# Head of a two-layer hybrid trunk: the first modulation computed in two halves by channels

## The chip, the cores and the metric

One core of a Trainium2 chip runs the whole program. The metric is the device time of one execution in microseconds (us). The kernel before took 1956.28 us, the median of 3 runs (1955.67 to 1959.99).

## The reference

Two groups of tokens (128 context tokens, 512 latent tokens, 1024 channels each) go through two layers with the same weights. Every layer first normalizes and modulates its input; the modulation comes from a small matrix product with a vector per group. Cut to what the change touches:

```python
for i in range(DEPTH):
    m = jax.nn.silu(cvec) @ P['ada_w'][i] + P['ada_b'][i]          # 1024 -> 6 * 1024
    sh1, sc1, g1, sh2, sc2, g2 = jnp.split(m[:, None, :], N_MOD, axis=-1)
    h = rmsnorm(x, P['norm_mix_g'][i]) * (1 + sc1) + sh1
    if i % 2 == 0:                                                 # layer 0: SSD || short convolution
        y, st = mixer_ssd_conv(h, P, e, h0)                        # u = h @ ssd_w_in, dt among its columns
    else:                                                          # layer 1: neighbourhood attention
        ...
    x = x + g1 * y
    h = rmsnorm(x, P['norm_ffn_g'][i]) * (1 + sc2) + sh2
    x = x + g2 * conv_ffn(h, P, i)
```

Nothing of layer 0's mixer can start before `sh1` and `sc1` of layer 0 are there: the first two sections of `ada_w[0]`, 1024 rows by 2048 columns of 4 bytes, 8.4 MB.

## The kernel before, in words

The activations lie in SBUF by channels: `C` = 8 chunks of 128 channels (the partitions) by `T` = 644 columns (128 context tokens, 4 columns of padding, 512 latent tokens). Every product with a large weight is done in three matmuls on a high and a low part: ScalarE copies a weight slot `raw` (128 x 1024) into `w_hi` (`split`, line 1087), GpSimd subtracts to get `w_lo` (`low`, line 550), and TensorE runs, for each chunk k and each half of the 644 columns, `w_hi*act_hi`, `w_hi*act_lo` and `w_lo*act_hi` (`half_slot`, lines 607, 608, 611). `raw` has two buffers, `w_hi` and `w_lo` four slots. The order of the work of each engine is written out by hand, with semaphores between the engines.

The head of the program runs so. SyncE's queue loads twelve small parameter arrays, then the eight row blocks of the first two sections of `ada_w`, 128 rows x 2048 columns each, into the tiles `first` (line 383), seven of them at once, since there are seven tiles. The eighth waits until TensorE is through with the first. Behind it the queue has the first two slots of `ssd_w_in` (`raw`, line 360), the table `na_rpb`, and the spill of `x`. ScalarE's queue loads the tokens `tok`, the dt weights `wdt`, and three small vectors `dtb`, `dld`.

TensorE transposes the tokens into PSUM in eight steps (lines 701, 702); VectorE copies each step to `x` (lines 1499, 1500). ScalarE has squared the tokens meanwhile and takes the roots; VectorE inverts them. `norm_spread(0)` (lines 657, 660) spreads the inverses over the partitions, and ScalarE copies them to `rinv` (line 1113). TensorE then sums the modulation over the eight blocks, four groups of 32 array columns at a time (line 707, bank 7). ScalarE copies the sums to `arow` (line 1166), TensorE turns them into columns (line 714), and VectorE adds the bias, `mod`, and forms `scale_a` (lines 1548, 1551).

VectorE had normalized all eight chunks before (`xn`, line 1511), added `dskip` (line 1515) and made the `masks` for the attention of layer 1 (lines 1519 to 1531). Then the eight chunks are modulated: for each, ScalarE writes `act_hi` (line 1169, two pieces, one for each group of tokens), and the unrounded value goes to `nt`, by VectorE for the even chunks (line 1561) and by ScalarE for the odd ones (line 1169); VectorE subtracts to get `act_lo` (line 1567). TensorE follows chunk by chunk: six matmuls for dt (lines 724 to 726) and six for the first tile of `ssd_w_in` (slot 0). ScalarE splits slots 0 and 1 between the chunks and slots 2 and 3 behind them.

Behind the chunks TensorE does tiles 1, 2 and 3 (slots 1 to 3). A tile goes into one of two pairs of PSUM banks, so tile 3 needs the banks of tile 1, which ScalarE frees (`tile_free1`) with the second of its two copies of tile 1 in `conv_in` (lines 1194, 1195). ScalarE takes these after tile 0's convolution: `zs` (line 1197) waits for VectorE's convolution of tile 0 (lines 1684, 1685), and VectorE comes to it only after it has built the table `tab` (15 copies, line 1654) and computed dt by a series (lines 1661 to 1677).

The names that matter below: `first_summed` (sums of the blocks done), `first_copied`, `first_turned`, `mod_ready`, `scale_ready`; `x_scaled` (a chunk of `xn` is there); `act_high`, `nt_ready`, `act_ready` (a chunk is ready for TensorE); `low_split` (a slot's `w_lo` is there).

## Time and profile before

| | us |
|---|---|
| median of 3 runs (lowest, highest) | 1956.28 (1955.67, 1959.99) |
| the profiled execution, own time | 1957.59 |
| its span in the profile | 1955.8 |
| TensorE busy in it | 1895.7 (97%) |
| VectorE, ScalarE, GpSimd busy | 1031.5, 672.0, 634.9 |
| mean granted TensorE clock | 0.985 of full |

All times of a row are counted from the start of the profiled span. In a row of a timeline the first number is the start, the second the time from the start of the first instruction to the end of the last of the row, and in square brackets stands how long the engine was idle before it and what ended that. Matmuls are pipelined, so a row's time is longer than the distance to the next row's start. The granted clock is 1.00 at 2.4 GHz and 0.50 at 1.2 GHz. The span is divided by the page into 40 slices of 49 us; everything that the change touches lies in the first two.

### The profile page before, as it was taken

The numbers are of one execution on the slowest core, as the hardware profiler recorded it, in microseconds if no ns is written. First come the engines' busy times: TensorE is split into PE (matmuls) and PEld (weight loads), VectorE is DVE, ScalarE is ACT, GpSimd is POOL, SyncE is SP. The second block draws the span as 40 slices with busy tenths as digits, with TensorE's granted clock in tenths as the row PEclk, the third lists the DMA queues.
The fourth block names the chain that finished last, engine by engine and source line by source line (L and its number), as shares of the span: only waits on it lengthen the run. The fifth ranks groups of instructions, "written<-read, shape, count | busy, mean of one in ns | idle before, by whom it ended". The sixth has DMA issues, their size and how long they took to land.

```text
span 1955.8 us, 35222 instructions
## 1 busy us (share of the span) xinstructions
PE 1895.7 (97%) x13425; PEld 1813.6 (93%) x13425; DVE 1031.5 (53%) x1987; ACT 672.0 (34%) x1021; POOL 634.9 (32%) x309
## 2 busy tenths in 40 slices
...
DMA packets 272884, 192.48 MB, mean 98 GB/s; under 512 B 25370, under 2 KB 259222, under 8 KB 271270
## 3 DMA queue, kind: packets, MB, share of 16 engines
...
## 4 chain that ended last, share of the span: by engine, by line
PE 86%; issue 5%; ACT 2%; DVE 2%; POOL 2%; DMA 2%; SPq 0%; POOLq 0%; ACTq 0%; DVEq 0%
PE ps L607 25%; PE ps L611 25%; PE ps L608 25%; PE ps L679 2%; POOL w_lo L550 2%; PE ps L1034 1%; PE ps L1014 1%; PE ps L856 1%; PE ps L999 1%; DVE act_lo L1595 1%; ACT sp L1386 1%; PE ps L686 0%; DMA x<-x_spill 0%; PE ps L1053 0%; PE ps L841 0%
## 5 line engine op out<-in xcount | busy, mean ns | idle before, releaser
L550 POOL TENSOR_TENSOR w_lo<-raw,w_hi 128x1024 fp32r<-128x1024 f32 x244 | 598.6, 2456 | 1229.6 <-ACT w_hi L1087 1229.6
L607 PE MATMUL ps<-act_hi,w_hi 128*128 128x322 f32 x2752 | 847.3, 315 | 6.6 <-DVE act_lo L1595 2.6
L608 PE MATMUL ps<-act_lo,w_hi 128*128 128x322 f32 x2624 | 802.4, 312 | 0.0
L611 PE MATMUL ps<-act_hi,w_lo 128*128 128x322 f32 x2752 | 635.6, 312 | 0.0
L607 PEld LDWEIGHTS ps<-act_hi,w_hi 128*128 128x128 f32 x2752 | 524.9, 191 | 20.4 <-issue 14.6
L608 PEld LDWEIGHTS ps<-act_lo,w_hi 128*128 128x128 f32 x2624 | 498.2, 190 | 0.0
L611 PEld LDWEIGHTS ps<-act_hi,w_lo 128*128 128x128 f32 x2752 | 465.8, 189 | 0.0
L1087 ACT ACTIVATE w_hi<-raw 128x1024 fp32r<-128x1024 f32 x244 | 256.1, 1051 | 370.2 <-PE ps L611 327.2
L607 PE MATMUL ps<-f_hi,w_hi 128*128 128x322 f32 x704 | 214.2, 311 | 0.0
L608 PE MATMUL ps<-f_lo,w_hi 128*128 128x322 f32 x704 | 213.7, 310 | 0.0
L1886 DVE SCALAR_TENSOR_TENSOR x<-ps,mod,x 128x128 f32 (+1 forms) x144 | 54.4, 433 | 265.8 <-PE ps L611 265.2
L611 PE MATMUL ps<-f_hi,w_lo 128*128 128x322 f32 x704 | 161.9, 311 | 0.0
L607 PEld LDWEIGHTS ps<-f_hi,w_hi 128*128 128x128 f32 x704 | 133.5, 190 | 0.0
L608 PEld LDWEIGHTS ps<-f_lo,w_hi 128*128 128x128 f32 x704 | 132.8, 189 | 0.0
L1685 DVE SCALAR_TENSOR_TENSOR ft<-fg,par,ft 128x644 f32<-128x644 f32 x44 | 123.6, 2810 | 7.8 <-DVE ft L1684 7.5
L611 PEld LDWEIGHTS ps<-f_hi,w_lo 128*128 128x128 f32 x704 | 118.0, 188 | 0.0
L1923 DVE TENSOR_TENSOR fg<-ps,spread 128x644 f32<-128x644 f32 x44 | 36.5, 830 | 132.2 <-PE ps L611 121.8
L1346 ACT ACTIVATE fe<-ft,gb 128x130 f32<-128x130 f32 x88 | 44.9, 557 | 127.4 <-DVE ft L1685 127.4
L1342 ACT ACTIVATE ft<-fg,par 128x644 f32<-128x644 f32 x44 | 36.7, 834 | 127.4 <-DVE fg L1923 127.3
L1495 DVE TENSOR_TENSOR acc<-acc,sq 128x644 f32<-128x644 f32 x40 | 58.2, 1455 | 19.9 <-ACT sq L1098 19.9
L1684 DVE SCALAR_TENSOR_TENSOR ft<-fg,par,ft 128x644 f32<-128x644 f32 x44 | 43.3, 984 | 44.3 <-ACT ft L1342 43.8
L1350 ACT ACTIVATE f_hi<-fa 128x644 f32 x44 | 32.7, 743 | 95.1 <-DVE fa L1935 95.1
...
## 6 DMA issues: line engine op xcount, KB each, us to landing
...
raw<-in_ssd_w_in SPq DMA_DIRECT2D x44, 512.0 KB, 3.8
raw<-in_ffn_w_gate SPq DMA_DIRECT2D x44, 512.0 KB, 3.7
raw<-in_ffn_w_up SPq DMA_DIRECT2D x44, 512.0 KB, 3.7
...
raw<-in_na_w_qkv SPq DMA_DIRECT2D x24, 512.0 KB, 3.7
...
first<-in_ada_w SPq DMA_DIRECT2D x8, 1024.0 KB, 13.0
```

The lines of the kernel that those rows point to most:

```text
L550: g.tensor_tensor(w_lo[:, s], raw[:, s % RAW], w_hi[:, s], ALU.subtract).then_inc(S["low_split"], 1)
L607: t.matmul(out, hi, chunk_of(src_hi, k0 + k, cols), start=start, stop=False)
L608: t.matmul(out, hi, chunk_of(src_lo, k0 + k, cols), start=False, stop=False)
L611: mm = t.matmul(ps[:, 2 * tset + h, 0:HALF], lo, chunk_of(src_hi, k0 + k, cols), start=False, stop=stop)
L679: mm = t.matmul(ps[g:g + ADA_COLS, bank, :], csil_w[:, 2 * q + k, :], ada[:, k, b * ADA_N:b * ADA_N + ADA_N], start=(q == 0), stop=(q == A ...
L1087: a(w_hi[:, s], raw[:, s % RAW], ACT.Copy).then_inc(S["high_split"], 1)
L1342: a(ft[k][:], fg[k][:, 1:T + 1], ACT.Copy, scale=w1).then_inc(S["ffn_mid"], 1)
L1346: ins = a(fe[k][:, lo:hi], ft[k][:, lo:hi], ACT.Gelu_apprx_tanh, bias=gb[:, k, stream:stream + 1])
L1495: tt(acc[:], acc[:], sq[:], ALU.add).then_inc(S["squares_used"], 1)
L1684: st.then_wait(stt(dst[:], buf[:, 0:T], w[:, bass.ds(w0, 1)], dst[:], ALU.mult, ALU.add))
L1685: return stt(dst[:], buf[:, 2:T + 2], w[:, bass.ds(w2, 1)], dst[:], ALU.mult, ALU.add)
L1886: ins = stt(dst, ps[:, 2 * k + bank, lo:hi], gate, dst, ALU.mult, ALU.add)
```

## The change

The two sections are taken in two halves by channels: columns 0 to 511 of both sections first, then columns 512 to 1023. Each of the seven tiles `first` would hold two half blocks (`quarters`); one tile is dropped, so there are twelve places. SyncE's queue loads eight half blocks of half 0 (128 partitions x 2 runs of 512 elements), then slot 0 of `ssd_w_in`, then eight half blocks of half 1 (the last four wait for the first sums), then slot 1.

On TensorE, `first_sum(0, s)` stands behind each of the eight steps of transposition, `norm_spread(0)` and `first_turn(0)` behind them. The loop over the chunks begins once half 0 of the modulation is there; the sums of half 1 stand behind chunks 0, 1 and 2 (three, three, two), and `first_turn(1)` behind chunk 3. Chunk 4 waits for `mod_ready`.

On ScalarE the copy of half 0's sums comes before `inverse(0)`, then the split of slot 0, then chunks 0 to 3; at chunk 4 the copy of half 1's sums, the split of slot 1, and chunks 4 to 7. The exponential of `dtb`, with the load of its table, moves from ahead of the chunks to behind them, before the splits of slots 2 and 3.

On VectorE `half_modulation` does `mod` and `scale_a` of four chunks at a time, into bank 4's columns; `xn` is no longer made for all chunks ahead but one chunk ahead of its use, inside the loop. `dskip` moves behind the chunks (before `tab`), the masks behind the first four convolutions.

```diff
-        first += [nc.alloc_sbuf_tensor_at(f"first{5 + n}", [P, 4, ADA_N], F32, offset=first_lo_at + n * 2 * C * P * 4) for n in range(2)]
+        first += [nc.alloc_sbuf_tensor_at("first5", [P, 4, ADA_N], F32, offset=first_lo_at + 2 * C * P * 4)]
+        quarters = [f[:, 2 * q:2 * q + 2, :] for f in first for q in range(2)]
...
-            for n in range(C):
-                if n >= len(first):
-                    sp.wait_ge(S["first_summed"], n - len(first) + 1)
-                sp.dma_start(first[n % len(first)][:], ada_w[0, n * P:n * P + P, 0:4 * ADA_N].rearrange("p (b n) -> p b n", b=4)
-                             ).then_inc(S[f"first_loaded{n}"], 16)
-            for s in range(RAW):
+            for n in range(2 * C):
+                if n == C:
+                    weights(SLOT_IN, 0, 0, rows(w_in, 0, C, U_BC))
+                if n >= len(quarters):
+                    sp.wait_ge(S["first_summed"], n - len(quarters) + 1)
+                src = bass.AP(tensor=ada_w.tensor, offset=(n % C) * P * MODS * D + (n // C) * ADA_N, ap=[[MODS * D, P], [D, 2], [1, ADA_N]])
+                sp.dma_start(quarters[n % len(quarters)], src).then_inc(S[f"first_loaded{n}"], 16)
+            for s in range(1, RAW):
...
+            def first_sum(half, k):
+
+                n = half * C + k
+                pe.wait_ge(S[f"first_loaded{n}"], 16)
+                for b in range(4):
+                    cols = slice(b % 2 * 2 * P, b % 2 * 2 * P + 2 * P)
+                    mm = t.matmul(ps[ADA_COLS * b:ADA_COLS * b + ADA_COLS, 3 if half else 7, 0:2 * P], csil_w[:, k, :],
+                                  quarters[n % len(quarters)][:, b // 2, cols], start=(k == 0), stop=(k == C - 1))
+                mm.then_inc(S["first_summed"], 1)
+
+            def first_turn(half):
+
+                pe.wait_ge(S["first_copied"], half + 1)
+                picks = ident[:].rearrange("p (b q) -> p b q", b=4)[:, :, 0:2]
+                for n in range(2):
+                    mm = t.matmul(ps[:, 4, 16 * half + 8 * n:16 * half + 8 * n + 8], arow[:, (2 * half + n) * P:(2 * half + n) * P + P], picks,
+                                  start=True, stop=True)
+                mm.then_inc(S["first_turned"], 1)
+
             for s in range(C):
                 if s >= 2:
                     pe.wait_ge(S["x_copied"], s - 1)
                 for n in range(LC):
                     t.transpose(ps[:, 5 + s % 2, n * P:n * P + P], tok[:, n, s * P:s * P + P], ident[:])
                 t.transpose(ps[:, s % 2, 0:P], tok[:, LC, s * P:s * P + P], ident[:]).then_inc(S["x_transposed"], 1)
+                first_sum(0, s)
             norm_spread(0)
-            for n in range(C):
-                pe.wait_ge(S[f"first_loaded{n}"], 16)
-                for b in range(4):
-                    mm = t.matmul(ps[ADA_COLS * b:ADA_COLS * b + ADA_COLS, 7, :], csil_w[:, n, :], first[n % len(first)][:, b, :],
-                                  start=(n == 0), stop=(n == C - 1))
-                mm.then_inc(S["first_summed"], 1)
-            pe.wait_ge(S["first_copied"], 1)
+            first_turn(0)
             pe.wait_ge(S["x_copied"], C)
-            picks = ident[:].rearrange("p (b q) -> p b q", b=4)[:, :, 0:2]
-            for n in range(4):
-                mm = t.matmul(ps[:, 5, 8 * n:8 * n + 8], arow[:, n * P:n * P + P], picks, start=True, stop=True)
-            mm.then_inc(S["first_turned"], 1)
-
-
             pe.wait_ge(S["wdt_ready"], 1)
-            pe.wait_ge(S["mod_ready"], 1)
             for k in range(C):
+                if k == 1:
+                    pe.wait_ge(S["rinv_ready"], 1)
                 pe.wait_ge(S["act_ready"], k + 1)
+                if k == C // 2:
+                    pe.wait_ge(S["mod_ready"], 1)
                 for h in range(2):
                     out, cols = ps[0:2 * HEADS, 5 + h, 0:HALF], slice(h * HALF, h * HALF + HALF)
                     t.matmul(out, wdt_hi[:, k, :], chunk_of(act_hi, k, cols), start=(k == 0), stop=False)
@@ -729,6 +744,10 @@
                 if k == 0:
                     slot_ready(SLOT_IN, 0, 0)
                 mm = half_slot(0, 0, [k], act_hi, act_lo, k == 0, k == C - 1)
+                for n in ((0, 1, 2), (3, 4, 5), (6, 7), ())[k] if k < 4 else ():
+                    first_sum(1, n)
+                if k == C // 2 - 1:
+                    first_turn(1)
...
+            act.wait_ge(S["first_summed"], C)
+            a(arow[:, 0:2 * P], ps[:, 7, 0:2 * P], ACT.Copy).then_inc(S["first_copied"], 1)
             inverse(0)
-            act.wait_ge(S["dskip_loaded"], 48)
-            a(dtb[:, 1, :], dtb[:, 1, :], ACT.Exp).then_inc(S["a_exp"], 1)
-            act.wait_ge(S["first_summed"], C)
-            a(arow[:], ps[:, 7, :], ACT.Copy).then_inc(S["first_copied"], 1)
+            split(SLOT_IN, 0, 0)
 
             def first_piece(dst, c, lo, hi, stream):
                 return a(dst, xn[:, c * T + lo:c * T + hi], ACT.Identity, scale=scale_a[:, c, stream:stream + 1],
                          bias=mod[:, 0, c, stream:stream + 1])
 
             for c in range(C):
-                if c == 0:
-                    act.wait_ge(S["scale_ready"], 1)
-                    act.wait_ge(S["x_scaled"], C)
+                if c == C // 2:
+                    act.wait_ge(S["first_summed"], 2 * C)
+                    a(arow[:, 2 * P:4 * P], ps[:, 3, 0:2 * P], ACT.Copy).then_inc(S["first_copied"], 1)
+                    for s in range(1, RAW):
+                        split(SLOT_IN, 0, s)
+                if c % (C // 2) == 0:
+                    act.wait_ge(S["half_ready"], c // (C // 2) + 1)
+                act.wait_ge(S["x_scaled"], c + 1)
                 for lo, hi, stream in STREAMS:
                     ins = first_piece(act_hi[:, c * T + lo:c * T + hi], c, lo, hi, stream)
                 ins.then_inc(S["act_high"], 1)
                 if c % 2 == 0:
                     if c > 0:
                         act.wait_ge(S["act_ready"], c)
+                    act.wait_ge(S["x_scaled"], c + 2)
                     for lo, hi, stream in STREAMS:
                         ins = first_piece(nt[:, 1, lo:hi], c + 1, lo, hi, stream)
                     ins.then_inc(S["nt_ready"], 1)
-                if c < RAW:
-                    split(SLOT_IN, 0, c)
+            act.wait_ge(S["dskip_loaded"], 48)
+            a(dtb[:, 1, :], dtb[:, 1, :], ACT.Exp).then_inc(S["a_exp"], 1)
...
-            for c0 in range(C):
-                tt(xn[:, c0 * T:c0 * T + T], x[:, c0 * T:c0 * T + T], rinv[:], ALU.mult).then_inc(S["x_scaled"], 1)
-            dve.wait_ge(S["dskip_loaded"], 48)
-            for h in range(2):
-                hp = slice(64 * h, 64 * h + 64)
-                ins = tt(dskip[hp, :], dld[hp, 0, h::2], dld[hp, 1, h::2], ALU.add)
-            st.did(ins)
-
...
-            st.wait()
-            dve.wait_ge(S["first_turned"], 1)
-            turned = ps[:, 5, 0:32].rearrange("p (n m h s) -> p m h n s", n=4, m=2, h=2)
-            for m in (1, 0):
-                adab = par[:, R_ADAB + m * C:R_ADAB + m * C + C].rearrange("p (h n) -> p h n", h=2).unsqueeze(3).broadcast_to([P, 2, 4, 2])
-                ins = tt(mod[:, m].rearrange("p (h n) s -> p h n s", h=2), turned[:, m], adab, ALU.add)
-                if m == 1:
-                    st.then_wait(ins)
-                    st.did(stt(scale_a[:], mod[:, 1], 1.0, bcast(par[:, R_NMIX:R_NMIX + C], 2, [P, C, 2]), ALU.add, ALU.mult))
-            ins.then_inc(S["mod_ready"], 1)
-            dve.wait_ge(S["mod_ready"], 1)
-            st.wait()
-            dve.sem_inc(S["scale_ready"], 1)
+            def half_modulation(half):
+
+                dve.wait_ge(S["first_turned"], half + 1)
+                turned = ps[:, 4, 16 * half:16 * half + 16].rearrange("p (n m h s) -> p m h n s", n=2, m=2, h=2)
+                at_ = slice(C // 2 * half, C // 2 * half + C // 2)
+                for m in (1, 0):
+                    adab = par[:, R_ADAB + m * C:R_ADAB + m * C + C][:, at_].rearrange("p (h n) -> p h n", h=2).unsqueeze(3).broadcast_to([P, 2, 2, 2])
+                    ins = tt(mod[:, m, at_].rearrange("p (h n) s -> p h n s", h=2), turned[:, m], adab, ALU.add)
+                    if m == 1:
+                        st.then_wait(ins)
+                        st.did(stt(scale_a[:, at_], mod[:, 1, at_], 1.0, bcast(par[:, R_NMIX:R_NMIX + C][:, at_], 2, [P, C // 2, 2]), ALU.add, ALU.mult))
+                if half == 1:
+                    dve.sem_inc(S["scale_ready"], 1)
+                    ins.then_inc(S["mod_ready"], 1)
+                    dve.wait_ge(S["mod_ready"], 1)
+                else:
+                    st.did(ins)
+                st.wait()
+                dve.sem_inc(S["half_ready"], 1)
+
+            def scaled_x(c):
+
+                tt(xn[:, c * T:c * T + T], x[:, c * T:c * T + T], rinv[:], ALU.mult).then_inc(S["x_scaled"], 1)
+
+            scaled_x(0)
             for c in range(C):
+                if c % (C // 2) == 0:
+                    half_modulation(c // (C // 2))
                 if c % 2 == 0:
                     if c > 0:
                         dve.wait_ge(S["act_ready"], c - 1)
+                    dve.wait_ge(S["x_scaled"], c + 1)
                     for lo, hi, stream in STREAMS:
                         st.did(ts(nt[:, 0, lo:hi], xn[:, c * T + lo:c * T + hi], scale_a[:, c, stream:stream + 1],
                                   mod[:, 0, c, stream:stream + 1], ALU.mult, ALU.add))
+                    scaled_x(c + 1)
                     st.wait()
                 else:
+                    if c < C - 1:
+                        scaled_x(c + 1)
                     dve.wait_ge(S["nt_ready"], c // 2 + 1)
...
             new_sum()
 
+            dve.wait_ge(S["dskip_loaded"], 48)
+            for h in range(2):
+                hp = slice(64 * h, 64 * h + 64)
+                ins = tt(dskip[hp, :], dld[hp, 0, h::2], dld[hp, 1, h::2], ALU.add)
+            st.did(ins)
+
             st.then_wait(v.memset(tab[:], 0.0))
...
             dve.wait_ge(S["sums_exp"], 1)
             st.did(tt(sc[:, :, K_END, :], sc[:, :, K_END, :], sc[:, :, K_DT, :], ALU.mult))
+            dve.wait_ge(S["consts_ready"], 2)
+            st.then_wait(v.tensor_single_scalar(qi[:, 0:1], qi[:, 0:1], QW - 1, ALU.bitwise_and))
...
+                st.then_wait(stt(masks[:, n, :], dist, float(QW - 1), ok, ALU.is_le, ALU.mult))
+                ins = ts(masks[:, n, :], masks[:, n, :], 1.0, BIG, ALU.subtract, ALU.mult)
+                st.did(ins)
+            st.wait()
```

## Rows read from the trace of the kernel before

**Rows 1.** The page: the chain that ended last, shares of the span by engine.

```profile
PE 86%; issue 5%; ACT 2%; DVE 2%; POOL 2%; DMA 2%; SPq 0%; POOLq 0%; ACTq 0%; DVEq 0%
```

**Rows 2.** Tile `first`: its DMA issues (duration ns, first and last start) and landings.

```profile
L383 SPq DMA_DIRECT2D first<-in_ada_w x8: 328/451/506, 6.1 to 25.2; - x8
...
DMA to landing us min/median/max: 7.6/13.0/20.3
```

**Rows 3.** DMA issues of 0 to 45 us: count, KB each, median us to landing.

```profile
raw<-in_ssd_w_in SPq DMA_DIRECT2D x3, 512.0 KB, 9.9
...
wdt<-in_ssd_w_in ACTq DMA_DIRECT2D x1, 128.0 KB, 22.9
```

**Rows 4.** Timeline of TensorE, 14 to 41 us.

```profile
22.25 0.66 PE L701 MATMUL ps<-ident,tok 128*128 128x128 f32 x4 [0.92 <-DVE x L1500]
...
23.07 1.06 PE L660 MATMUL ps<-ident,roots 128*128 128x128 f32 x8
24.06 6.35 PE L707 MATMUL ps<-first,csil_w 128*32 128x512 f32 x56
33.91 1.93 PE L707 MATMUL ps<-first,csil_w 128*32 128x512 f32 x8 [3.50 <-DMA first<-in_ada_w]
36.55 1.88 PE L714 MATMUL ps<-ident,arow 128*128 128x8 f32 x8 [0.72 <-ACT arow L1166]
```

**Rows 5.** Timeline of TensorE's weight loads, 24 to 38 us.

```profile
24.05 0.16 PEld L707 LDWEIGHTS ps<-first,csil_w 128*32 128x32 f32 x8
```

**Rows 6.** Windows: length, busy us (count) of PE, PEld, DVE, ACT, POOL; granted clock, DMA share, GB/s.

```profile
33.90:38.00 4.10, 3.38 (x15) 1.65 (x15) 2.32 (x13) 0.60 (x1) 0.00 (x0) 0.50 1.12 427
49.00:50.00 1.00, 1.00 (x6) 0.92 (x6) 1.00 (x3) 0.08 (x1) 0.00 (x0) 0.66 0.94 244
```

**Rows 7.** Timeline of VectorE, 24 to 130 us.

```profile
25.88 6.01 DVE L1511 TENSOR_TENSOR xn<-x,rinv 128x644 f32<-128x644 f32 x8 [0.23 <-ACT rinv L1113]
32.28 0.34 DVE L1515 TENSOR_TENSOR dskip<-dld 64x8 f32<-64x8 f32 x2 [0.39 <-DMA dld<-in_ssd_d]
...
38.55 0.17 DVE L1548 TENSOR_TENSOR mod<-ps,par 128x16 f32<-128x16 f32 x1 [1.97 <-PE ps L714]
...
39.20 0.80 DVE L1561 TENSOR_SCALAR nt<-xn,scale_a,mod 128x128 f32<-128x128 f32 x2 [0.18 <-DVE mod L1548]
...
43.57 1.93 DVE L1567 TENSOR_TENSOR act_lo<-nt,act_hi 128x644 fp32r<-128x644 f32 x1 [2.30 <-ACT act_hi L1169]
...
55.59 0.83 DVE L1567 TENSOR_TENSOR act_lo<-nt,act_hi 128x644 fp32r<-128x644 f32 x1 [0.86 <-ACT act_hi L1169]
...
58.25 4.08 DVE L1654 COPY tab<-tabr 16x31 f32<-16x31 f32 x15
...
99.99 0.89 DVE L1684 SCALAR_TENSOR_TENSOR cgs<-gpad,halfw,cgs 128x644 f32<-128x644 f32 x1 [6.35 <-ACT gpad L1195]
```

**Rows 8.** Timeline of GpSimd, 24 to 130 us.

```profile
42.46 5.27 POOL L550 TENSOR_TENSOR w_lo<-raw,w_hi 128x1024 fp32r<-128x1024 f32 x2 [38.80 <-ACT w_hi L1087]
```

**Rows 9.** Timeline of ScalarE, 24 to 130 us.

```profile
25.26 0.59 ACT L1113 ACTIVATE rinv<-ps 128x512 f32<-128x512 f32 x1
25.86 1.28 ACT L1164 ACT_TABLE_LOAD   x1
...
39.14 1.20 ACT L1169 ACTIVATE act_hi<-xn,mod,scale_a 128x128 fp32r<-128x128 f32 x2 [2.64 <-DVEq L1555]
...
41.33 1.04 ACT L1087 ACTIVATE w_hi<-raw 128x1024 fp32r<-128x1024 f32 x1
...
74.37 0.70 ACT L1195 ACTIVATE gpad<-ps 128x644 f32<-128x644 f32 x1
```

**Rows 10.** Timeline of TensorE, 40 to 130 us.

```profile
44.87 0.63 PE L607 MATMUL ps<-act_hi,w_hi 128*128 128x322 f32 x1 [1.66 <-POOL w_lo L550]
...
60.98 0.41 PE L607 MATMUL ps<-act_hi,w_hi 128*128 128x322 f32 x1
...
75.32 0.31 PE L607 MATMUL ps<-act_hi,w_hi 128*128 128x322 f32 x1
```

28 lines of the change are left out of this document (12 added, 16 removed).

## Prediction

> **What bounds the kernel now.** I read the page's chain first: 86% of it is TensorE [rows 1], so a head that ends earlier is worth something only if TensorE's unbroken run of tiles starts earlier. Next the loads. Seven row blocks of 1 MB are queued from 6.1 us, one every 0.45 us; the first lands 7.6 us after its issue (13.7), the seventh 20.3 after (29.1) [rows 2], so one MB takes 2.6 us, and the eighth ends TensorE's wait at 33.9 [rows 4]. Then the engines of the head: the sums take 1.93 us, the turn 1.88 [rows 4], VectorE's first modulation comes at 38.55 [rows 7], chunk 0's `act_hi` at 39.14 [rows 9], TensorE's first tile at 44.87 [rows 10]. The reader is to see that the eighth block sets all this.
>
> Then I ask what the run behind hangs on. The last chunk's `act_lo` ends at 55.59 + 0.83 = 56.42 [rows 7], tile 1 starts at 60.98 and tile 3 at 75.32 [rows 10], 7.17 us a tile, 0.149 us a matmul. Tile 3 needs tile 1's banks, which ScalarE's copy frees at 74.37 + 0.70 = 75.07 [rows 9]: only 0.25 us before TensorE wants them. That copy stands behind VectorE's chain: last `act_lo`, the table's copies (to 58.25 + 4.08 = 62.33 [rows 7], 5.91 us behind that `act_lo`), dt, the convolution of tile 0. So two paths arrive together at 75.1 to 75.3, and the one over VectorE has nearly no slack. The change pays only where it brings the last `act_lo` forward.
>
> **Loads and sums of half 0.** Half blocks are 0.5 MB, 1.3 us each; eight land by 13.7 - 1.3 + 7 x 1.3 = 21.5. I take 22.5 for the eighth, since runs of 2 KB have no row here; bounds 21.5 and 25. Slot 0 follows with 0.5 MB: 24 to 25.
>
> The sums of half 0 move between the transpositions. Seven blocks took 6.35 us [rows 4], 0.9 each with the drain and a short wait counted in; I take 0.86 at full clock and twice that at half (the eighth: 1.93 with its drain). Its eight weight loads issue in 0.16 us [rows 5], so loads do not set its pace, columns do, and a half block costs 0.43 or 0.86; bounds 0.2 and 0.9. Eight add 4.3 to the transpositions, partly in waits that were there (0.92 before the last step [rows 4]). I take +1.3 (bounds 0 and 4.5): the last sum ends at 24.15 instead of the transpositions at 22.85. `norm_spread` takes 1.3, to 25.3, and `first_turn(0)`, four records of the eight in 1.88, 0.5 at full clock: 25.8. `rinv` is there 0.65 us behind the spread [rows 9], 25.95.
>
> wdt lands 22.9 us after its issue, at 24.8, though it is 128 KB [rows 3]: it shares the DMA engines with row blocks whose runs are 8 KB. ScalarE copies it ahead of half 0's sums. With it landing at 24.8 again, the turn ends 0.3 later, and that is the bound I keep. The Trainium skill (DMA: Bandwidth & Descriptors, Queues, rings and completion order) has each engine go round its queues a packet at a time. By that wdt would land earlier beside runs of 2 KB, and those 0.3 us go.
>
> **Chunks 0 to 3.** VectorE: `xn` of chunk 0 takes 0.75 (6.01 for eight [rows 7]), 26.0 to 26.75; half 0's modulation to 27.3. ScalarE splits slot 0 from 26.0 to 27.0 (1.04 [rows 9]), and GpSimd subtracts for about 2.4 us, to 29.45. While GpSimd did that before (42.46 to 47.73 [rows 8]) VectorE's `act_lo` took 1.93 instead of 0.83 [rows 7]: the one waits for the other. So `nt` of chunk 0 starts at 29.45: 0.80 + 0.75 (`xn` of chunk 1) + 0.8 = 31.8, and TensorE starts at 31.9 with slot 0 there, 9.5 us before dt's first matmul and 13 before tile 0's.
>
> But it starts at the low clock. A pause of 3.5 us before 33.91 left the granted clock at 0.50 [rows 4, 6]; here it is 25.8 to 31.9. Before, from the start at 44.87 the clock came back within 49 to 50, whose mean is 0.66 [rows 6]: at 49.7, 4.8 us. I take 4.8 again. In them go chunk 0's twelve matmuls (12 x 0.27 = 3.2) and 1.9 half blocks of sums; at full clock remain 36 x 0.149 = 5.4 and 6.1 x 0.43 = 2.6. End of chunk 3: 31.9 + 4.8 + 8.0 = 44.7, the last sum 1.8 before, 42.9. Half 1 has landed by about 34, so it does not bind; VectorE's chunks 1 to 3 (2.3 us each with `xn` among them) are ready by 39, and don't either.
>
> **The second modulation** is the new wait. `first_turn(1)` 0.5, to 45.2; the first add 0.17 [rows 7]. Meanwhile ScalarE: copy of the sums 0.35, split of slot 1 1.04, to 44.3, and GpSimd holds 44.4 to 46.8. `scale_a` reads two operands from SBUF and falls in there. I let it wait: half 1 ready at T = 47.1. No row shows so small an instruction in this place; bounds T = 46.0 (not held) and 47.1. The Trainium skill (SBUF — State Buffer, SBUF: two separate sides) says that a VectorE instruction with both inputs in SBUF fully blocks while a GpSimd one that reads SBUF runs, and that one reading PSUM is not held; by it the add passes and `scale_a` waits, T = 47.1, and a VectorE free of it would give 46.0, 1.1 us less on the whole. The 1.93 us row agrees for the long ones.
>
> **Chunks 4 to 7.** Per pair VectorE has `nt` 0.80 and `xn` 0.75; then ScalarE, which waits for that `xn`, does `nt` and `act_hi` of the odd chunk, 1.1 each (two pieces in 1.20 with the drain [rows 9]), and `act_lo` 0.85: 4.65. Two pairs: the last `act_lo` ends at T + 9.3 = 56.4, against 56.42. TensorE, idle from 45.2 to T + 2.4 = 49.5, is at the low clock once more and ends tile 0 near 59; ScalarE has exponential, table load 1.28 [rows 9] and splits 2 and 3 to 59.1, then dt's copy, so tile 1 starts near 60.4, 0.6 earlier than now.
>
> **Moved pieces.** The masks leave VectorE's stretch between 32.62 and 36.58 (3.96 us, the idle 1.97 before 38.55 counted off [rows 7]), where they lay under the loads: gain 0. They go into 6.35 us of idle before the convolution at 99.99 [rows 7]: 0, and 2.4 to spare; if that cover shrank below 3.96 the difference would hit the convolutions. `dskip` goes onto VectorE's chain: +0.34 [rows 7]. The table load leaves a stretch in the loads' shadow and delays splits 2 and 3 by 1.5; slot 2 is wanted at 67: 0. SP's queue: slot 0 passes eight half blocks (it lands at 25 instead of 35), slot 1 none; the spill of `x` behind them waits for nobody.
>
> **Sum.** VectorE's path: 0.0 + 0.34; the banks of tile 1 come at 75.4. TensorE's path wants them at 74.7, and waits. Tile 3 at 75.4 instead of 75.32: +0.1. Made against the profiled execution, 1957.59 becomes 1957.7; against the median 1956.28, 1.3 below that execution, it is 1956.4. The lead of 9 to 13 us at chunk 0 is spent on sums among the chunks, `xn` inside the loop (a pair 4.65 instead of 3.3 of ScalarE alone), and a second stop of about 4 us for the second modulation.
>
> **Rivals.** (a) *Second modulation early*: `scale_a` isn't held, TensorE's clock is up by 35. T = 44.9 to 45.5, change 0.34 - 1.9 - 0.25: -1.8, 1954.5. For it: pauses so far differ. Against: the low clock behind 3.5 us of pause. (b) *The lead is handed on*: slot 0's subtraction and the clock both cost nothing, chunk 3 ends at 31 + 10.5 = 41.5, T = 42: last `act_lo` 51.3, -4.8, 1951.5. Against: rows 7 and 8. (c) *Slower, by the clock*: with the matmuls of chunks 0 to 3 all at half pace, 12.9 + 6.9 = 19.8 us, chunk 3 ends at 51.7, T = 52.2 to 54.2 and the gate moves +5.5 to +7: 1962.5. It decides against me once the clock stays down past about 41, nine us after the start. Against: 4.8 us before. (d) *Slot 0 is late*: before, the slots landed 9.9 us (median) after issue [rows 3]. ScalarE's split stands ahead of chunk 0, so if slot 0 lands at 31 or later instead of 25, all of it moves by 5: +5, 1961.4; then the change doesn't do what it says.
>
> **Chances.** Forecast 0.65 (own range 1955 to 1959.5: bounds of the sums, half blocks and T), a 0.14, b 0.07, c 0.08, d 0.06. The range for 8 in 10 is 1953.6 to 1960.2. About 0.2%, 3.9 us, is what a measurement of this kernel tells from no change, so faster means under 1952.4 and slower over 1960.2: faster is b and a little of a, 0.09; slower c and most of d, 0.13; same 0.78.
>
> **What would show it.** Right: half 0's last sum near 24; dt's first matmul at 31 to 33; granted clock 0.50 there and full by 38; TensorE idle about 4 us behind chunk 3; `scale_a` of half 1 as GpSimd's subtraction ends; last `act_lo` at 56 to 57; TensorE idle a moment before tile 3, released by ScalarE's copy. Wrong: a last `act_lo` before 53 or past 60, tile 3 away from 75.4 by over 3 us, or a convolution behind tile 4 that waits for masks.

## The result, and the profile after

The changed kernel is slower: 1965.68 us (median of 7 runs, 1960.6 to 1967.22) against 1957.78 (median of 7, 1955.67 to 1959.99) for the kernel before in the same session, ratio 1.0037 with a 95% interval of 1.0027 to 1.0048. The forecast was 1956.4, the range 1953.6 to 1960.2, so the time lies outside it, on the side that had a chance of 0.13. The profiled execution took 1965.73 us, its span is 1963.9, and TensorE was busy for 1897.0 us of it, 1.3 more than before: the other 6.8 of the 8.1 us are idle time of TensorE. The chain of the page is again TensorE's.

The landing of the first small loads, which TensorE's first matmul waits for, moves from run to run (11.58 to 12.39 us into the span over 19 profiles; 11.67 in the profile before, 12.39 in this one). So where two kernels are compared I count from that first matmul ("behind the first matmul").

The page's chain of the kernel after, the issues of DMAs of 0 to 45 us (count, KB each, median us to landing) and the landings of tile `first` [rows 1, 3, 2]:

```profile
PE 87%; issue 5%; DVE 2%; POOL 2%; ACT 2%; DMA 1%; SPq 0%; POOLq 0%; ACTq 0%; DVEq 0%
```

```profile
raw<-in_ssd_w_in SPq DMA_DIRECT2D x3, 512.0 KB, 12.4
...
wdt<-in_ssd_w_in ACTq DMA_DIRECT2D x1, 128.0 KB, 14.8
```

```profile
DMA to landing us min/median/max: 7.5/10.9/13.7
```

The loads bound nothing, as forecast: wdt came 14.8 us behind its issue instead of 22.9, and nothing in this head waited for it or for a half block. That queues are served in turn is what the Trainium skill (DMA: Bandwidth & Descriptors, Queues, rings and completion order) says; by that rule wdt had to come earlier beside shorter runs, and the trace agrees. The losses start on TensorE. Its timeline after [rows 4, 10]:

```profile
24.97 0.64 PE L707 MATMUL ps<-first,csil_w 128*32 128x256 f32 x8
...
26.23 0.64 PE L707 MATMUL ps<-first,csil_w 128*32 128x256 f32 x8
...
28.02 0.51 PE L716 MATMUL ps<-ident,arow 128*128 128x8 f32 x4
...
34.35 0.45 PE L739 MATMUL ps<-act_hi,wdt_hi 128*32 128x322 f32 x1 [5.82 <-DVE act_lo L1585]
...
37.67 2.42 PE L707 MATMUL ps<-first,csil_w 128*32 128x256 f32 x24
...
45.23 1.07 PE L707 MATMUL ps<-first,csil_w 128*32 128x256 f32 x16
...
48.03 0.51 PE L716 MATMUL ps<-ident,arow 128*128 128x8 f32 x4
52.80 0.33 PE L739 MATMUL ps<-act_hi,wdt_hi 128*32 128x322 f32 x1 [4.26 <-DVE act_lo L1585]
...
63.24 0.49 PE L756 MATMUL ps<-ident,dtrow 32*128 32x32 f32 x5 [1.13 <-ACT dtrow L1226]
...
80.41 0.49 PE L611 MATMUL ps<-act_hi,w_hi 128*128 128x322 f32 x1 [2.21 <-ACT gpad L1219]
```

A step of five transpositions and four sums repeats every 1.265 us (23.70, 24.97, 26.23) with no idle between. Then come the two stops, 5.82 and 4.26 us, both released by VectorE's `act_lo`, and a third of 2.21 us ahead of tile 3, released by ScalarE's copy, where the kernel before had none [rows 10]. VectorE, GpSimd and ScalarE after [rows 7 to 9]:

```profile
30.18 2.54 DVE L1576 TENSOR_SCALAR nt<-xn,scale_a,mod 128x128 f32<-128x128 f32 x2 [0.15 <-DVE mod L1550]
...
48.58 0.17 DVE L1550 TENSOR_TENSOR mod<-ps,par 128x8 f32<-128x8 f32 x1 [7.08 <-PE ps L716]
48.78 1.36 DVE L1553 SCALAR_TENSOR_TENSOR scale_a<-mod,par 128x8 f32<-128x8 f32 x1
...
59.27 0.83 DVE L1585 TENSOR_TENSOR act_lo<-nt,act_hi 128x644 fp32r<-128x644 f32 x1 [1.75 <-ACT act_hi L1187]
...
60.81 0.34 DVE L1672 TENSOR_TENSOR dskip<-dld 64x8 f32<-64x8 f32 x2
61.40 0.86 DVE L1675 MEMSET tab<- 16x960 f32 x1 [0.25 <-issue]
62.29 5.23 DVE L1678 COPY tab<-tabr 16x31 f32<-16x31 f32 x15
...
106.77 0.89 DVE L1708 SCALAR_TENSOR_TENSOR cgs<-gpad,halfw,cgs 128x644 f32<-128x644 f32 x1 [4.13 <-ACT gpad L1219]
```

```profile
29.84 2.34 POOL L554 TENSOR_TENSOR w_lo<-raw,w_hi 128x1024 fp32r<-128x1024 f32 x1 [26.17 <-ACT w_hi L1106]
47.77 2.35 POOL L554 TENSOR_TENSOR w_lo<-raw,w_hi 128x1024 fp32r<-128x1024 f32 x1 [15.59 <-ACT w_hi L1106]
61.74 4.74 POOL L554 TENSOR_TENSOR w_lo<-raw,w_hi 128x1024 fp32r<-128x1024 f32 x2 [11.62 <-ACT w_hi L1106]
```

```profile
59.18 1.28 ACT L1210 ACT_TABLE_LOAD   x1
...
60.61 1.99 ACT L1106 ACTIVATE w_hi<-raw 128x1024 fp32r<-128x1024 f32 x2
62.51 0.68 ACT L1226 ACTIVATE dtrow<-ps 32x644 f32<-32x644 f32 x1
...
79.57 0.70 ACT L1219 ACTIVATE gpad<-ps 128x644 f32<-128x644 f32 x1
```

The reader is to lay the three over one another. GpSimd runs from 29.84, 47.77 and 61.74; in each of these stretches VectorE has an instruction that is far too long: `nt` 2.54 instead of 0.80, `scale_a` 1.36 instead of 0.17, and the 15 copies of the table 5.23. That the add of `mod` at 48.58 took 0.17 beside GpSimd while `scale_a` behind it was held agrees with the Trainium skill (SBUF — State Buffer, SBUF: two separate sides) on one and two operands from SBUF. The number of operands does not tell it all: `nt` and the table's copies read one tile each in SBUF and were held too, 2.54 us instead of 0.80 and 5.23 instead of the 1.35 that they take with GpSimd idle (below). For comparison, GpSimd's pair of subtractions behind the last chunk in the kernel before, where the last `act_lo` ends at 56.42 [rows 7]:

```profile
56.52 4.76 POOL L550 TENSOR_TENSOR w_lo<-raw,w_hi 128x1024 fp32r<-128x1024 f32 x2 [8.78 <-ACT w_hi L1087]
```

It starts 0.10 us behind that `act_lo`; in the changed kernel the pair starts at 61.74, 1.64 behind an `act_lo` that ends at 60.10.

The granted clock (columns as in rows 6):

```profile
80.41:84.41 4.00, 4.00 (x17) 4.00 (x18) 3.16 (x3) 1.51 (x2) 0.85 (x1) 0.57 0.45 122
...
34.30:39.00 4.70, 4.65 (x28) 3.19 (x32) 3.74 (x7) 3.30 (x7) 0.00 (x0) 0.50 1.13 396
39.00:44.00 5.00, 5.00 (x57) 3.05 (x50) 1.49 (x2) 1.57 (x3) 0.00 (x0) 0.94 0.98 393
52.80:57.00 4.20, 4.20 (x18) 3.40 (x19) 3.19 (x6) 2.81 (x6) 0.00 (x0) 0.59 0.12 35
```

It is low behind both long stops, as forecast, and low once more, 0.57 over four us, behind the third; four us behind the start of tile 3 have 1.00 in the kernel before.

### The profile page after: what moved, and what is told of

The parts are those of the page before. It is cut to its first block, busy times and chain, and to the rows that moved or that the text cites. A ratio compares the mean times of both kernels' runs of the same rounds, so it can differ in the third digit from the quotient of the medians.

```text
span 1963.9 us, 35373 instructions
## 1 busy us (share of the span) xinstructions
PE 1897.0 (97%) x13489; PEld 1813.8 (92%) x13489; DVE 1033.1 (53%) x1990; ACT 672.5 (34%) x1022; POOL 634.9 (32%) x309
## 4 chain that ended last, share of the span: by engine, by line
PE 87%; issue 5%; DVE 2%; POOL 2%; ACT 2%; DMA 1%; SPq 0%; POOLq 0%; ACTq 0%; DVEq 0%
PE ps L611 25%; PE ps L615 25%; PE ps L612 25%; PE ps L683 2%; POOL w_lo L554 2%; PE ps L1053 1%; PE ps L1033 1%; PE ps L875 1%; PE ps L1018 1%; DVE act_lo L1613 1%; ACT sp L1410 1%; PE ps L707 1%; DMA x<-x_spill 1%; PE ps L690 0%; PE ps L795 0%
```

## The experiments

Two points hold for all. "The gate" is ScalarE's copy of tile 1's banks, which frees them for tile 3. Positions in the table are us behind the first matmul of each profile; each kernel was timed against the kernel before in turns, in 5 rounds, or 3 for the first four; `before_p1`, `before_p2`, `after_p1` and `after_p2` are single profiles. The first four columns come from one profile each, the ratio from all executions, and an execution that was profiled can stand at either end of its kernel's times: that of `warm` took 1961.9 (median 1958.78), that of `sums_early` 1958.25 (median 1961.67).

| kernel | last `act_lo` ends | table's copies take | tile 3 starts | idle ahead of it | ratio, 95% interval |
|---|---|---|---|---|---|
| before; before_p1; before_p2 | 44.75; 43.58; 42.83 | 4.08; 4.14; 4.09 | 63.65; 62.43; 62.22 | 0; 0.19; 0 | 1 |
| after | 47.71 | 5.23 | 68.02 | 2.21 | 1.0037 (1.0027, 1.0048) |
| after_again | 47.37 | 5.24 | 67.69 | 2.25 | 1.0045 (1.0031, 1.0059) |
| after_p1; after_p2 | 47.16; 47.67 | 5.21; 5.23 | 67.47; 67.99 | 2.20; 2.22 | |
| before_late | 43.47 | 1.35 | 63.99 | 1.86 | 1.0017 (1.0007, 1.0027) |
| tab_idle | 47.03 | 1.35 | 65.62 | 0.49 | 1.0029 (1.0018, 1.0040) |
| warm | 46.04 | 5.22 | 66.34 | 2.19 | 1.0014 (1.0003, 1.0025) |
| sums_early | 45.29 | 5.23 | 65.61 | 2.25 | 1.0026 (1.0016, 1.0035) |
| second_fast | 42.87 | 5.23 | 63.19 | 2.21 | 1.0008 (0.9999, 1.0017) |
| no_table | 41.68 | 1.35 | 59.87 | 1.04 | 0.9996 (0.9987, 1.0005) |
| no_table_warm | 41.67 | 1.35 | 59.86 | 1.04 | 0.9993 (0.9983, 1.0002) |
| before_tab_moved | 44.71 | 1.35 | 63.63 | 0 | 0.9999 (0.9990, 1.0008) |
| after_tab_moved | 47.71 | 1.35 | 66.31 | 0.49 | 1.0023 (1.0012, 1.0033) |
| sums_behind | 47.11 | 5.24 | 67.43 | 2.22 | 1.0036 (1.0024, 1.0049) |
| exp_idle | 48.27 | 1.36 | 68.52 | 2.36 | 1.0035 (1.0021, 1.0049) |
| exp_dskip_idle | 48.28 | 4.09 | 67.09 | 1.94 | 1.0038 (1.0026, 1.0050) |

**Is it the gate?** The first two runs load and unload VectorE's chain and leave the rest alone. `before_late` repeats the clear of the table four times; `tab_idle` does the table ahead of the second modulation, where VectorE waits 7.08 us.

```diff
-            st.then_wait(v.memset(tab[:], 0.0))
+            for _ in range(5):
+                st.then_wait(v.memset(tab[:], 0.0))
```

> The kernel before, with four more clears of `tab` (0.86 us each, 3.5 us in all) on VectorE ahead of the table's copies; nothing else. Theory G: the gate has 0.25 us of slack there, so tile 3 starts 3.2 us later (78.5 instead of 75.3 us), TensorE idles just before it, released by ScalarE's copy to `gpad`, and perhaps runs on at the low clock for some us (up to 1.6 more): 1961.0 to 1962.6 against 1957.8. Rival W: VectorE has room there, the time stays at 1957.8.

```diff
+                if c == C // 2:
+                    st.then_wait(v.memset(tab[:], 0.0))
+                    dve.wait_ge(S["table_loaded"], 16)
+                    for r in range(DR):
+                        st.did(v.tensor_copy(tab[:, DR - 1 - r, QW:QW + DC], tabr[:, r, DC - 1::-1]))
                 if c % (C // 2) == 0:
                     half_modulation(c // (C // 2))
...
-            st.then_wait(v.memset(tab[:], 0.0))
-            for r in range(DR):
-                st.did(v.tensor_copy(tab[:, DR - 1 - r, QW:QW + DC], tabr[:, r, DC - 1::-1]))
```

> The changed kernel, with the table for the attention (the clear of `tab` and its 15 copies) built in VectorE's idle stretch ahead of the second half's modulation (41.5 to 48.5 us in the changed kernel) instead of behind the last chunk. Theory G (the gate): tile 3 of the input product starts when ScalarE has freed tile 1's banks, and that stands behind VectorE's last `act_lo`, the table and dt. Without the table's 6.3 us on that path tile 3 should start when TensorE itself comes to it, at 78.1 instead of 80.4 us, without the 2.2 us of idle and without the low clock behind it (1.6 us): 3.9 us less than the changed kernel, 1961.8. Rival W (work): TensorE's own longer head sets the end, and VectorE's order is cover; then tile 1 and tile 3 start where they do now and the time stays at 1965.7.

VectorE, GpSimd and TensorE of `before_late`:

```profile
61.93 1.35 DVE L1655 COPY tab<-tabr 16x31 f32<-16x31 f32 x15
```

```profile
55.75 4.74 POOL L550 TENSOR_TENSOR w_lo<-raw,w_hi 128x1024 fp32r<-128x1024 f32 x2 [8.78 <-ACT w_hi L1087]
```

```profile
76.17 0.39 PE L607 MATMUL ps<-act_hi,w_hi 128*128 128x322 f32 x1 [1.86 <-ACT gpad L1195]
```

4.45 us of clears gave 1.86 us of idle and a ratio of 1.0017: slower, but less than expected (1959.93 us against 1961.0 to 1962.6). The reason is in the rows: the copies began behind GpSimd's end (55.75 + 4.74 = 60.49) and took 1.35 instead of 4.08, so the chain grew by 4.45 - 2.73 = 1.7. This is the first sight of what the copies cost: alone 1.35. In `tab_idle` they took 1.35 too, tile 3 came 1.9 to 2.4 us earlier than in the profiles of the changed kernel, and of the idle 0.49 was left; its median, 1961.57, is the 1961.8 that was expected. Both agree with the gate, and with a time that follows it.

**Where does the chain lose?** `warm` puts transpositions of the identity (46 behind `first_turn(0)`, 34 behind `first_turn(1)`), whose results nobody reads, into the two stops, so that the clock stays up. `sums_early` takes half 1's sums four and four behind chunks 0 and 1, and its turn behind chunk 2.

```diff
             first_turn(0)
+            filler(46)
...
                     first_turn(1)
+                    filler(34)
```

> The changed kernel, with transpositions of the identity into an unused part of bank 7 as filler in TensorE's two pauses (46 behind the first turn, 34 behind the second), to keep its clock up. Theory G with the low clock as one of its parts: chunk 0 to 3 run at the full clock from the start, 2.3 us shorter, the second half's modulation, the last `act_lo` and the gate come 2.3 us earlier (tile 3 at 78.1), and the time is 1963.4. Rival D (VectorE and ScalarE pace chunks 0 to 3, the clock is only a symptom): chunk 3 ends less than 1 us earlier and the time stays above 1965. A second pause before tile 3 stays in either case.

```diff
-                for n in ((0, 1, 2), (3, 4, 5), (6, 7), ())[k] if k < 4 else ():
+                for n in ((0, 1, 2, 3), (4, 5, 6, 7), (), ())[k] if k < 4 else ():
...
-                if k == C // 2 - 1:
+                if k == C // 2 - 2:
```

> The changed kernel, with the eight sums of half 1 behind chunks 0 and 1 (four each) instead of 0, 1 and 2, and the second turn behind chunk 2 instead of chunk 3, so that chunk 3's matmuls lie beside the second modulation. Half 1's last block lands at about 37 us and is needed at 43. Theory G: the half's modulation, the last `act_lo` and tile 3 come 1.7 us earlier, the idle before chunk 4 shrinks from 4.3 to about 2.5 us, and the time is 1964.0 or, where the shorter pause also keeps the clock up, 1963. Rival W: TensorE does the same work in another order, tile 1 starts when it does now, 1965.7.

`warm` brought the last `act_lo` 1.1 to 1.7 us forward, and its time came down by more than that (1958.78, against 1963.4 expected); where the rest of it comes from is not shown. `sums_early` brought it 1.9 to 2.4 forward (1961.67, against 1963 to 1964). In both the idle ahead of tile 3 stayed at 2.2: the gate keeps its distance to the last `act_lo`. ScalarE's copy ends 20.2 us behind it, and tile 3 starts 20.3 behind it, in each of the profiles of the changed kernel and of these two; in the three of the kernel before the copy ends 18.7 behind it, and tile 3 starts 0.1 to 0.7 after the copy. `after_again` is the changed kernel once more.

> The changed kernel, unaltered, for its time beside the same runs of the kernel before as the three that follow, and for a second profile. Both theories: 1.0037 times the kernel before; tile 3 starts 68 us after TensorE's first matmul, with about 2 us of idle ended by ScalarE's copy to `gpad`. A profile whose head differs by over 1 us in that distance would say that single profiles don't carry differences of that size.

It gave 1.0045, tile 3 at 67.69. `second_fast` adds to `sums_early` the split of slot 1 ahead of the wait for half 1's sums, so that GpSimd does not hold `scale_a`, and `xn` of chunks 5 to 7 in VectorE's idle.

```diff
+                    for s in range(1, RAW):
+                        split(SLOT_IN, 0, s)
                     act.wait_ge(S["first_summed"], 2 * C)
                     a(arow[:, 2 * P:4 * P], ps[:, 3, 0:2 * P], ACT.Copy).then_inc(S["first_copied"], 1)
-                    for s in range(1, RAW):
-                        split(SLOT_IN, 0, s)
...
+                if c == C // 2:
+                    for ahead in range(c + 1, C):
+                        scaled_x(ahead)
```

> The changed kernel with the sums of half 1 behind chunks 0 and 1 and the second turn behind chunk 2, slot 1 split on ScalarE ahead of the copy of half 1's sums (its subtraction then ends before `scale_a`), and `xn` of chunks 5 to 7 made in VectorE's idle stretch ahead of the second modulation. Theory G: half 1 is there 2.9 us earlier, chunks 4 to 7 take 7.5 instead of 9.8 us, the last `act_lo` ends 41.7 us after TensorE's first matmul (47.7 in the changed kernel), and tile 1 starts 3.6 us earlier than in the kernel before. But the table (with GpSimd beside it) and dt still stand ahead of the gate: tile 3 starts about 63 us after the first matmul as in the kernel before (63.65), with 2 us of idle and the low clock behind it. Ratio 0.9995 to 1.0005. Rival W (TensorE's own work and pauses in the head decide): the 3.6 us come through, ratio 0.998.

The last `act_lo` came 4.3 to 4.8 us earlier than in the changed kernel, tile 1 at 46.4 instead of 50.7 to 51.3, and tile 3, as much earlier, at 63.19. Against the kernel before, tile 1 is 1.3 to 2.9 us early and tile 3 is not: 2.21 us of idle still stand ahead of it. The ratio, 1.0008, cannot be told from 1. `no_table` is built on `second_fast` and takes the table's clear and copies out of the chain, behind the first four convolutions, and ScalarE copies dt's rows and takes the exponential between the splits of slots 2 and 3; `no_table_warm` adds 46 and 14 transpositions of the identity to it.

```diff
-            st.then_wait(v.memset(tab[:], 0.0))
-            dve.wait_ge(S["table_loaded"], 16)
-            for r in range(DR):
-                st.did(v.tensor_copy(tab[:, DR - 1 - r, QW:QW + DC], tabr[:, r, DC - 1::-1]))
...
             st.did(tt(sc[:, :, K_END, :], sc[:, :, K_END, :], sc[:, :, K_DT, :], ALU.mult))
+            st.then_wait(v.memset(tab[:], 0.0))
...
```

> As the one before, with the table built behind the first four convolutions (ahead of the masks) and ScalarE's copy of dt's rows and the exponential between the splits of slots 2 and 3. Theory G: the gate is lifted; dt's chain starts as soon as dt's rows are turned, tile 3 starts 60.4 us after TensorE's first matmul, with at most 0.5 us of idle before it; 3.3 us less than the kernel before, ratio 0.9983, and at least 2 us less than the kernel of the run before this one. If the table and the copies are not what holds the gate, this kernel and that of the run before agree within 1 us.

> As the one before, with filler transpositions in TensorE's two pauses (46 behind the first turn, 14 ahead of chunk 4) to hold its clock. Both theories take the low clock over the first chunk for a cost of 1.7 us: ratio 0.9974. If the clock had only hidden VectorE's pace there (a chunk every 2.3 us), it stays within 0.7 us of the run before it.

Tile 3 of `no_table`:

```profile
71.80 0.38 PE L611 MATMUL ps<-act_hi,w_hi 128*128 128x322 f32 x1 [1.04 <-ACT gpad L1221]
```

Tile 3 comes at 59.87 (expected 60.4), 2.4 to 3.8 us ahead of the three profiles of the kernel before. The times show 0.4 and 0.7 in a thousand, where 1.7 and 2.6 were expected, each interval with 1.0 in it. `no_table_warm` has no low clock from its first chunk to behind tile 3 (0.50 in `no_table` from 31.4 to 38.2 us), and yet its last `act_lo` (41.67) and its tile 3 (59.86) stand where they do in `no_table`: the 1.7 us that I put on the clock there were not on the path to tile 3. So these heads are early, but no version was shown to beat the kernel before, and 2 us or so of the lead are not found again in the time.

**The table alone.** The same move of the table in the kernel before and in the changed kernel.

> The kernel before with one change: VectorE's clear and 15 copies of the table (1.1 + 4.08 us between the last act_lo and dt's chain) move behind the first four convolutions. Theory G (tile 3 starts at the later of two arrivals: TensorE's own run of tiles, or VectorE's chain with ScalarE's second copy): before, the two arrive 0.25 us apart, so VectorE 5.2 us earlier gives 0.25 us and no more; tile 3 at 63.4 to 63.6 behind TensorE's first matmul (63.65 before), no idle ahead of it, ratio 0.9998, within 0.9990 to 1.0005. Theory V (the time follows VectorE's chain of the head one for one): -5 us, 0.9974.

> The changed kernel with the same move of the table and nothing else. Theory G: tile 1 starts where it does in the changed kernel (51.3 to 51.9 us behind TensorE's first matmul), the two tiles take 14.3, so tile 3 comes 65.6 to 66.3 behind it instead of 67.7 to 68.0, without the idle of 2.2 ahead of it and without the low clock behind that idle: 2.2 + up to 1.6 less than the changed kernel, ratio to the kernel before 1.0025 to 1.0033 instead of 1.0037 to 1.0045. Theory T (the late start of tile 1 is the whole loss, the table's copies are harmless): as the changed kernel, 1.004. Theory U (the table's copies are most of the loss): 1.0015 or less.

```profile
78.20 0.39 PE L611 MATMUL ps<-act_hi,w_hi 128*128 128x322 f32 x1 [0.49 <-ACT gpad L1219]
```

In the kernel before, 5 us off VectorE's chain left tile 3 at 63.63 and the time where it was: TensorE's own tiles set the start. In the changed kernel the same edit moved tile 3 from 67.5 to 68.0 to 66.31 (the row above) and the ratio to 1.0023 (1.0025 to 1.0033 expected). Theory G stands; the late start of tile 1 is the larger part of the loss, the copies the smaller.

**The pace of the mixed steps.** `sums_behind` puts all 32 sums of half 0 behind the transpositions.

```diff
-                first_sum(0, s)
+            for s in range(C):
+                first_sum(0, s)
```

> The changed kernel with half 0's 32 sums behind the eighth transposition instead of four behind each. Theory M (the pace of the mixed steps, 1.27 us, is TensorE's own work: 0.5 us and more a half block on top of a transposition, which no wait absorbs): the transpositions end 10.8 to 11.4 us behind the first matmul, eight half blocks take 3.5 to 4.3 more, the last sum ends at 14.4 to 15.4 behind it (14.4 in the changed kernel), and the time is the changed kernel's within 1 us, 1.0035 to 1.005. Theory X (it is the alternation of transpositions and 32-column sums that costs): sums alone at 0.43 beside a transposition pace of before, last sum at 13.5 or earlier, and 1 us less in time.

```profile
22.41 0.66 PE L724 MATMUL ps<-ident,tok 128*128 128x128 f32 x4 [0.48 <-DVE x L1525]
...
23.11 3.66 PE L707 MATMUL ps<-first,csil_w 128*32 128x256 f32 x64
```

Alone, eight half blocks take 3.66 us, 0.457 each, and the last ends 14.9 behind the first matmul against 14.5 in the changed kernel (14.1 to 15.2 over its four profiles), not 13.5 or earlier: theory M. Mixing in costs 0.11 a step and gives back the waits; the sums are work of 3.7 us wherever they stand.

**Why the copies end late.** In the kernel before GpSimd's pair of subtractions starts 0.10 us behind the last `act_lo`, in the changed kernel 1.64 behind, since ScalarE's exponential and table load now come first. Two of the 15 copies wait, each for the end of one subtraction: single copies last up to 2.35 and 2.38 us, the others 0.16. `exp_idle` runs the exponential in ScalarE's idle ahead of half 1's sums (first diff); `exp_dskip_idle` moves dskip's adds as well, into VectorE's idle (second).

```diff
                 if c == C // 2:
+                    act.wait_ge(S["dskip_loaded"], 48)
+                    a(dtb[:, 1, :], dtb[:, 1, :], ACT.Exp).then_inc(S["a_exp"], 1)
                     act.wait_ge(S["first_summed"], 2 * C)
```

```diff
                 if c == C // 2:
+                    dve.wait_ge(S["dskip_loaded"], 48)
+                    for h in range(2):
+                        hp = slice(64 * h, 64 * h + 64)
+                        ins = tt(dskip[hp, :], dld[hp, 0, h::2], dld[hp, 1, h::2], ALU.add)
+                    st.did(ins)
```

> The changed kernel with one thing back: the exponential of dtb, with its table load (1.28 + 0.23 us), runs in ScalarE's idle 5.8 us ahead of the copy of half 1's sums, and no longer between the last chunk and the splits of slots 2 and 3. Theory L (the step that the forecast priced at nothing: these 1.5 us make GpSimd's subtractions of slots 2 and 3 start 1.64 us behind the last act_lo instead of 0.10, and VectorE's copies of the table end 1.05 us behind the second subtraction, whenever they start): the last act_lo stays at 47.2 to 47.7 behind the first matmul, GpSimd starts 0.1 us behind it, the copies take less than 4.3 us and end 6.0 to 6.3 us behind the last act_lo (7.4 in the changed kernel), dt's rows and tile 1 come up to 1.4 us earlier too, tile 3 at 66.3 to 66.8 (67.5 to 68.0), the idle ahead of it stays at about 2; ratio 1.0026 to 1.0040. Theory N (ScalarE's place for it doesn't matter): copies 5.23, tile 3 at 67.5 to 68.0, ratio as the changed kernel's.

> exp_idle, and dskip's two adds with it, ahead of the second modulation in VectorE's idle 7 us. In exp_idle these adds (both operands in SBUF) fell behind the start of GpSimd's two subtractions and took 4.15 us instead of 0.34, so the table's copies still ended 7.4 us behind the last act_lo. Theory H (whatever of VectorE's small work stands behind the last act_lo is held once GpSimd runs, and only the order of the two edits' pieces cost that 1.5 us): the sequence of the kernel before is back, the copies take 4.1 and end 5.8 to 6.0 us behind the last act_lo, tile 3 comes 1.4 to 1.6 us earlier against the last act_lo than in the changed kernel (20.3 behind it there, 18.7 to 18.9 here), the idle ahead of it stays near 2 us or goes to 0.6; ratio 1.0024 to 1.0038. Theory N: 20.3 again, and the changed kernel's ratio.

VectorE of `exp_idle`, then of `exp_dskip_idle`:

```profile
60.90 4.15 DVE L1672 TENSOR_TENSOR dskip<-dld 64x8 f32<-64x8 f32 x2
65.30 0.86 DVE L1675 MEMSET tab<- 16x960 f32 x1 [0.25 <-issue]
66.19 1.36 DVE L1678 COPY tab<-tabr 16x31 f32<-16x31 f32 x15
```

```profile
61.19 0.86 DVE L1675 MEMSET tab<- 16x960 f32 x1 [0.26 <-DVE acc L1636]
62.08 4.09 DVE L1678 COPY tab<-tabr 16x31 f32<-16x31 f32 x15
```

`exp_idle` refuted my account of it: GpSimd did start 0.10 behind the last `act_lo`, but now dskip's adds fell behind its start and took 4.15 us instead of 0.34, and the copies ended 7.37 behind that `act_lo`, as in the changed kernel (7.42). With both pieces out, the copies end 5.92 behind it and tile 3 comes 18.81 behind it (expected 18.7 to 18.9; 20.3 in the changed kernel). The ratios, 1.0035 and 1.0038, don't show these 1.5 us: in both profiles the last `act_lo` ended 0.6 to 1.1 us later than in the four profiles of the changed kernel, and the intervals are 0.0024 and 0.0028 wide.

**Profiles repeated.** Tile 3 is 4.0 to 4.4 us later against the profile that I forecast from, the medians differ by 7 to 9. Two more profiles of each kernel:

> The changed kernel unaltered, for its profile alone, beside one of the kernel before. So far tile 3 comes 4.0 to 4.4 us later behind TensorE's first matmul (63.65 before), while the medians of the times differ by 7.3 to 8.8. From tile 3 to the end of the span three profiles of kernels with the old head take 1879.5 to 1880.8 (mean 1880.3), ten with the new head 1878.8 to 1883.8 (mean 1881.7). Theory S (the rest is scatter of low-clock spells that fall on both kernels alike): tile 3 at 67.5 to 68.1 behind the first matmul, the stretch behind tile 3 in 1879 to 1884, its mean over the repeats within 1 us of the old kernel's. Theory R (the new head sets off a spell of its own further back): the mean stretch 2 us or more longer than the old kernel's, and the granted clock shows the same place in each of its profiles.

> As after_p1: S says 1879 to 1884 from tile 3 to the end with the old kernel's mean, R 2 us or more above that mean.

> The kernel before unaltered, for its profile alone. Tile 3 at 63.4 to 64 behind TensorE's first matmul. Theory S: the stretch from tile 3 to the end spreads over 1879 to 1884 as in the changed kernel. Theory R: it stays at 1879.5 to 1881.

> As before_p1: S says 1879 to 1884 from tile 3 to the end, R 1879.5 to 1881.

TensorE in `before_p2`, and the granted clock behind tile 3 in `after_p2` and `after_again`:

```profile
33.12 1.06 PE L707 MATMUL ps<-first,csil_w 128*32 128x512 f32 x8 [2.61 <-DMA first<-in_ada_w]
34.90 1.50 PE L714 MATMUL ps<-ident,arow 128*128 128x8 f32 x8 [0.72 <-ACT arow L1166]
```

```profile
80.28:84.28 4.00, 4.00 (x17) 4.00 (x18) 3.16 (x3) 1.52 (x2) 0.84 (x1) 0.57 0.43 117
```

```profile
79.47:83.47 4.00, 4.00 (x27) 4.00 (x28) 3.16 (x3) 1.50 (x2) 0.86 (x1) 1.00 0.45 118
```

Two things come out. First, the profile of the kernel before on which the forecast rests was its slowest head of three: the eighth block's sum took 1.93 us there at the low clock [rows 4] and 1.06 here, and the last `act_lo` ended at 44.75 against 43.58 and 42.83. Against the mean of the three, 62.8, tile 3 of the changed kernel (mean of four, 67.8) is 5.0 us late, not 4.0 to 4.4. Second, in three of the four profiles of the changed kernel the clock falls right behind the idle ahead of tile 3 (0.57 to 0.58 over 4 us, 1.00 in `after_again`), which costs about 1.7 us each time (17 matmul records in 4 us instead of 27), and in none of the four with the old head and its table where it was or moved. Counted at the second of ScalarE's two copies of tile 4 (to `gpad`), the mean is 92.6 (93.56, 90.16, 92.99, 93.49) against 86.2 (87.59, 86.52, 84.60): 6.3 us. The spans end 7.3 later, counted the same way. From tile 3 to that copy the four profiles of the changed kernel take 25.5, 22.5, 25.5 and 25.5, the three of the kernel before 23.9, 24.1 and 22.4: behind tile 3 a further stretch of low clock stands in both kernels, longer in some profiles (6.8 us) than in others (3.4). The two lowest, 22.5 and 22.4, are those with the short stretch and with full clock at tile 3, so the masks, which moved to there, cost nothing.

The stretch from tile 3 to the end is 2.3 us longer in the changed kernel in the mean (1882.9 against 1880.6), as theory R asked (2 or more), but "in each of its profiles" did not hold: `after_again` has no such spell. So theory R stands in part. Its numbers for the old head missed: tile 3 at 62.43 and 62.22 where 63.4 to 64 was expected, and 1878.9 to 1882.4 from there to the end; the last 1.0 us is within this scatter.

## Why the prediction was wrong

What held, step by step: the loads (the eighth half block and slot 0 bound nothing); the first `nt` and the second `scale_a` held by GpSimd; low clock behind the first stop, here to 39.6, 5.2 us from TensorE's start at 34.35 (4.8 was taken; 2.8 to 5.2 in the four profiles); a second stop of about 4 us (4.26) and low clock again; masks free, with 4.13 us of idle still ahead of the convolution; the gate as the place where the two paths meet. Of the rivals (c) came nearest with 1962.5, 3.2 short of the measured time, but by the clock alone, which did not stay down: chunk 3's turn ended at 48.5, where (c) has chunk 3 end at 51.7. Rivals (a), (b) and (d) did not come. Two of the signs that I had named for being wrong did: a last `act_lo` past 60 (60.10), and tile 3 over 3 us from 75.4 (80.41).

What failed is a set of sizes on one chain, and one term put at nothing. At the profiled execution the gate's copy ended at 79.57 + 0.70 = 80.27 where 75.4 was forecast, 4.9 us later:

- "I take +1.3 (bounds 0 and 4.5)": the sums among the transpositions. The last sum ended 14.5 us behind the first matmul, where the forecast has 24.15 - 11.67 = 12.5: **+2.0**. I let waits absorb 3 of 4.3 us, where the rows had 0.92 and little more; `sums_behind` shows 3.66 us of pure work. Of this, 1.7 was left at chunk 0's start.
- The first matmul itself came 0.72 later in this execution: scatter, no effect of the change.
- Chunks 0 to 3 with half 1's sums, from TensorE's start to the end of the turn: 34.35 to 48.54, 14.2 instead of 13.3: **+0.9** (a half block took 0.5 at full clock, not 0.43).
- From T to the last `act_lo`: 9.8 instead of 9.3: **+0.5**. The modulation between, 1.8 instead of 1.9: -0.1.
- "delays splits 2 and 3 by 1.5; slot 2 is wanted at 67: 0", and the table's copies "5.91 us behind that `act_lo`": **+1.2** (7.42, of which 0.34 was in the sum for dskip). I asked only who waits for slot 2, not what GpSimd's later start does to VectorE's chain. This is the step that was wrong in kind and not only in size: `exp_dskip_idle`, which takes the exponential and dskip's adds out of this place, has the copies end 5.92 behind the last `act_lo` again, as before.

The terms add up to 0.7 + 1.7 + 0.9 - 0.1 + 0.5 + 1.2 = 4.9. Behind that stands a term that the sum did not have: the idle that opens ahead of tile 3 (2.2 us) is followed by the low clock in three of four profiles, up to 1.7 us. That the idle is what brings it is not shown by an experiment of its own; no profile without such an idle has it. And the base was off: I worked against one profile as if the waits in its head were fixed, though the old head is 1.2 to 1.9 us shorter in two other profiles. With 0.25 us between the two paths at the gate nothing could be gained there and all could be lost; my own bound for the sums, 3.2 us above the value I took, pointed to slower, and the range still ended at 1960.2.
